# Unread 512-column products ahead of the scores in two attentions of a two-model kernel

## The chip, the cores and the metric

One Trainium2 chip, one core of it. The metric is device microseconds of one execution of the whole program; the state before is the median of three runs.

## The reference

The program computes a block of one model and then the two layers of a second one, for 256 tokens of width 1024 in float32: a mixing layer (gated linear attention, block attention, memory attention) with a hierarchical mixture of 32 experts; an even layer; an odd layer with sliding-window attention. Both later layers have modulation vectors ("ada") from a condition and a gated feed-forward part.

The change lies in the even layer, which has two attentions side by side on the same normed input:

```python
def _diff_attention(q, k, v, lam, slopes):        # 4 heads, two score maps each
    ...
        logits = jnp.einsum('bqhmd,bshmd->bhmqs', qi, k).astype(jnp.float32) * scale
        ...
        p = jax.nn.softmax(logits, axis=-1)
        a = p[:, :, 0] - lam * p[:, :, 1]
        return jnp.einsum('bhqs,bshe->bqhe', a.astype(v.dtype), v)

def _dsa_attention(q, k, v, iq, ik, iw, slopes, topk):   # 8 heads, keys chosen by an index score
    ...
        idx_logits = jnp.einsum('bqhd,bsd->bqhs', iqi, ik).astype(jnp.float32) * IDX_DIM ** -0.5
        score = jnp.einsum('bqhs,bqh->bqs', jax.nn.relu(idx_logits), iwi.astype(jnp.float32))
        score = jnp.where(causal[None], score, -jnp.inf)
        _, sel = lax.top_k(score, topk)
```

The second attends only to the chosen keys, with softmax and a distance penalty like the first.

## The kernel before, in words

Each engine has its own hand-written program; they meet at semaphores. Helpers record the instructions, so nearly all TensorE work has line 1826 (`mm`) or, for transposes, 1830 (`tr`), and nearly all VectorE and ScalarE work line 32.

*Attention as a pipeline.* An attention is a list of units. A unit is one block of 128 queries with two score maps (two maps of one head in attention 2, two heads in attention 3). A unit has 128 keys (first query block) or 256 (second). Attention 2 has eight units, alternately 128 and 256 keys; attention 3 has eight, first four with 128 keys, then four with 256. `attend(n, beside, ready)` runs `pipeline(...)`: at step t, TensorE does `turns` of unit t-3 (transposes of the softmaxed rows), `scores` of unit t and `values` of unit t-4 (product with v), in that order. VectorE at step t does `weights` of unit t-1 (adds the distance penalty, takes the row limit; waits for the scores), `norms` of unit t-2 (after ScalarE's exponential; these feed `turns`), the reading out of unit t-5, and side work.

*Banks of PSUM.* Scores of unit U go to banks 2(U%2) and 2(U%2)+1. `take(b)` waits until VectorE has read what was in the bank; the two score products read 64 rows each (rows 0 to 63 and 64 to 127 of the array).

*Side work.* `side.go(beside)` at the head of `scores` runs up to two pieces of other work: in attention 2 transposes of heads (`headturn`) and the index scores of attention 3 (`indexer`: two 64-row products, a relu by ScalarE, a weighted sum by VectorE, four times for each query block). VectorE's side work is the top-k selection (MAX8 and MATCH_REPLACE8 in rounds).

*Ada runs.* `ada(("u", n, u))` behind the scores computes modulation vectors of later stages: in units 0, 2, 4, 6 a run of eight float32 products of 512 columns (`ring,csr`, in the trace 16 instructions, four side by side at 32 columns of the array each), copied to `acc` by ScalarE; in units 1, 3, 5, 7 its closing: four float32 products of 1 column on `acc` (`ones,acc`, 8 instructions), read by VectorE into `modc`. A run waits for its weights in the ring of slots that SP's queue fills, and for VectorE's reading of bank 7.

*Operands.* `hH` (in the trace `hT_r`) holds the rounded, normed and modulated input of the layer, 8 chunks of 256 columns. After the projections nobody reads it in this layer's attentions; attention 3 writes its results to chunks 4 to 7. A product of two rounded operands is one instruction, one of two float32 operands two.

The names and lines of the change are in the TensorE program:

Of the kernel before, what the change touches and what calls it, by code (L numbers as in the profile page):

```python
# [113 lines left out]
def pipeline(n, *stages):  # L114
    for t in range(n + max(lag for lag, _ in stages)):
        for lag, stage in stages:
            if 0 <= t - lag < n:
                stage(t - lag)
# [118 lines left out]
def build(nc, A, out_ap, dbg):  # L237
    ctx = ExitStack()
    with ctx:
# [5 lines left out]
        def both(name, shape):  # L245
            with nc.sbuf_tensor(name + "_r", shape, FR) as rounded:
                pass
            return sb(name, shape), rounded
# [15 lines left out]
        hT, hH = both("hT", [128, 8, 256])  # L264
# [41 lines left out]
        _, WF = both("W_a", [128, 3072])  # L306
# [12 lines left out]
        _, WFc = both("W_c", [128, 3072])  # L319
# [4 lines left out]
        ps = [ctx.enter_context(nc.psum_tensor(f"ps{i}", [128, 512], FP)) for i in range(8)]  # L324
# [93 lines left out]
        for i in range(nch):  # L418
            if i == first["ak"]:
                last_use = {}  # L420
            b = min(range(3 if i in beside else 6), key=lambda z: (last_use.get(z, -1), z))
# [1391 lines left out]
        def tensor(pe):  # L1813
# [6 lines left out]
            def take(*banks):  # L1820
                for b in banks:
                    if b in free:
                        pe.wait_ge(*free.pop(b))

            def mm(out, lhsT, rhs, start, stop):
                return pe.matmul(out, lhsT, rhs, start=start, stop=stop, skip_group_check=True)  # L1826

            def tr(out, in_):
                n = in_.shape[0]
                return pe.transpose(out, in_, ident[0:n, 0:n])  # L1830

            def ada(point):
                for v, what in plan.rows.get(point, ()):
                    l, i, k = plan.ada_order[v]
                    take(7)
                    if what == "run":
                        w = ring[:, slot[k], :].rearrange("p (c n) -> p c n", c=8)
                        pe.wait_ge(*landed[k])
                        if v == 0:
                            pe.wait_ge(s_cs, 1)  # L1840
                        for c in range(8):
                            t = mm(ps[7][32 * (c % 4):32 * (c % 4) + 32, :], csr[:, c, :], w[:, c, :], c < 4, c >= 4)
                        t.then_inc(s_ar, 1)
                        free[7] = (s_acp, v + 1)
                        continue
                    pe.wait_ge(s_acp, v + 1)
                    if row_gate(l, i):
                        mm(ps[7][:, :], ones[:, :], acc[:, :], True, False)
                        mm(ps[7][:, :], ones[0:1, :], gates[0:1, 512 * (i % 2):512 * (i % 2) + 512], False,
                           True).then_inc(s_ac, 1)  # L1850
                        free[7] = C.next(s_gate)
                    else:
                        for n in range(4):
                            t = mm(ps[7][:, n:n + 1], acc[:, 128 * n:128 * n + 128], ones[:, 0:1], True, True)
                        t.then_inc(s_ac, 1)
                        free[7] = C.next(s_modc)
# [16 lines left out]
            def begin(i):  # L1873
                ada(("f", i))
# [117 lines left out]
            def attend(n, beside, ready):  # L1992
                at_n = attns[n]

                def scores(u):
                    U, unit = at_n.u0 + u, at_n.units[u]
                    side.go(beside)
                    if n == 3 and u == 4:
                        side.until(ev, "sel1")
                    for need in ready.get(u, ()):  # L2000
                        pe.wait_ge(*need)
                    for m in range(2):
                        b = 2 * (U % 2) + m
                        take(b)
                        mm(ps[b][:, 0:unit.nk], unit.q[m], unit.k[m], True, True).then_inc(s_sc, 1)
                        free[b] = (s_mx, 2 * U + m + 1)
                    ada(("u", n, u))

                def turns(u):
                    U, unit = at_n.u0 + u, at_n.units[u]  # L2010
                    b, n = 4 + U % 2, unit.nk // 128
                    take(b)
                    pe.wait_ge(s_nm, U + 1)
                    for i in range(unit.blocks):
                        o = 257 * (i // n) + 128 * (i % n)
                        t = tr(ps[b][:, 128 * i:128 * i + 128], at_n.pb[:, U % 4, o:o + 128])
                    t.then_inc(s_tr, 1)
                    free[b] = (s_cp, U + 1)

                def values(u):  # L2020
                    U, unit = at_n.u0 + u, at_n.units[u]
                    n, pT = unit.nk // 128, at_n.pT[:, U % 2, :]
                    if unit.first:
                        take(6)
                    pe.wait_ge(s_cp, U + 1)
                    if unit.lam is not None:
                        for i in range(n):
                            t = mm(ps[6][:, 0:128], pT[:, 128 * i:128 * i + 128], unit.v[0][i], i == 0, i == n - 1)
                        t.then_inc(s_pv, 1)
                    else:  # L2030
                        for i in range(n):
                            for m in range(2):
                                t = mm(ps[6][64 * m:64 * m + 64, 128 * unit.a:128 * unit.a + 128], unit.v[m][i],
                                       pT[:, 128 * (n * m + i):128 * (n * m + i) + 128], i == 0, i == n - 1)
                                if i == n - 1:
                                    t.then_inc(s_pv, 1)
                    if unit.last:
                        free[6] = (s_fin, at_n.fin[u])

                pipeline(len(at_n.units), (3, turns), (0, scores), (4, values))  # L2040


# [127 lines left out]
            attend(1, 1, {0: [(s_hv, 4)]})  # L2170
            side.end()
            ada(("o", 0))
            pe.wait_ge(s_gla, 8)
            pe.wait_ge(s_fin, t1.end)
# [388 lines left out]
```

## Time and profile before

| | us |
|---|---|
| median of 3 runs (1468.08 to 1469.96) | 1469.69 |
| the profiled execution | 1468.73 |
| its span, first to last instruction | 1467.0 |
| TensorE busy, whole program | 1191.2 (81%) |
| VectorE busy | 615.8 (42%) |
| ScalarE busy | 475.6 (32%) |
| mean granted clock of TensorE (1.00 is 2.4 GHz) | 0.88 |

Times in the trace are microseconds from the first instruction. PE is TensorE, PEld its weight loads, DVE VectorE, ACT ScalarE. PEclk is the mean granted clock of a stretch: 0.50 is the low level, 1.2 GHz. Matmuls overlap in a pipeline, so the cost of one in a series is the distance between starts, not its length. The chain is followed back from the last instruction, at each step to what released it.

### The profile page before, as it was taken

The page shows a single profiled execution, that of the slowest core. Times are in us where ns is not written, and L with a number is a line of the kernel's source. Part 1 is how long each engine was busy: PE and PEld are TensorE (multiplying, and loading weights), DVE is VectorE, ACT ScalarE, POOL GpSimd, SP SyncE. Part 2 cuts the span into 40 slices and gives each one's busy share as a digit, 9 for nine tenths or more (in the row PEclk, how much of TensorE's full clock was granted, in tenths as well). Part 3 has the DMA queues.
Part 4 walks back from the last instruction along what each step waited for, and adds up shares of the span by engine and source line. Part 5 has one row for each costly group of instructions (what it writes and reads, how often), then busy time and mean ns, then how long its engine had stood idle before and what let it go on. Part 6 is the DMA issues. An engine that isn't in the chain of part 4 may idle for free.

```text
span 1467.0 us, 19464 instructions
## 1 busy us (share of the span) xinstructions
PE 1191.2 (81%) x7703; PEld 874.9 (60%) x7703; DVE 615.8 (42%) x1240; ACT 475.6 (32%) x767; POOL 7.6 (1%) x54
## 2 busy tenths in 40 slices
PE   5888888575676756846897888999999978999998
PEld 4665565242332323413675438899898735999986
DVE  3473652010010000101663676655535656565553
ACT  4561621000000000002532335555433447455541
POOL 1000000000000000000000000000000000000000
PEclk9897888798888878978897678899999988999999
DMA  8542149999999999999446431865546472655520
GB/s 294 173 150 80 59 168 424 430 429 430 431 429 428 431 430 428 431 425 401 164 152 244 172 116 58 264 204 203 191 151 223 174 274 70 222 181 187 205 98 29
DMA packets 121729, 368.67 MB, mean 251 GB/s; under 512 B 9842, under 2 KB 56093, under 8 KB 110878
## 3 DMA queue, kind: packets, MB, share of 16 engines
q1 hardware_dynamic: 120556, 367.26, 65.1%
q8 instruction: 64, 1.05, 0.3%
q10 hardware_dynamic: 1074, 0.08, 0.1%
q14 instruction: 35, 0.29, 0.1%
HBM read 366.28 MB, written 1.05 MB: 250 GB/s over the span
## 4 chain that ended last, share of the span: by engine, by line
PE 57%; DMA 22%; DVE 12%; ACT 5%; issue 3%; SPq 1%; DVEq 0%; ACTq 0%
PE ps L1826 54%; DMA more<-in_w_gate_dram 8%; DMA more<-in_w_down_dram 7%; DMA more<-in_w_up_dram 6%; PE ps L1830 3%; DVE st L32 3%; DVE ring_r L32 2%; DVE R_c L32 2%; SPq L669 1%; DVE X_c L32 1%; DVE R_a L32 1%; DVE X_a L32 1%; ACT W_c_r L32 1%; ACT X_c L32 1%; DVE sc L32 1%
## 5 line engine op out<-in xcount | busy, mean ns | idle before, releaser
L1826 PE MATMUL ps<-hT_r,ring_r 128*128 128x256 f32 x864 | 243.7, 282 | 0.0
L1826 PE MATMUL ps<-ring,xg 128*32 128x512 f32 x640 | 140.1, 734 | 126.1 <-DMA more<-in_w_gate_dram 79.3
L1826 PEld LDWEIGHTS ps<-ring,xg 128*32 128x32 f32 x640 | 36.9, 132 | 222.3 <-issue 222.3
L1826 PEld LDWEIGHTS ps<-hT_r,ring_r 128*128 128x128 f32 x864 | 166.0, 192 | 0.0
L32 DVE TENSOR_TENSOR ring_r<-ring,W_c_r 128x1024 fp32r<-128x1024 f32 x94 | 115.2, 1225 | 96.3 <-ACT W_c_r L32 92.4
L1826 PE MATMUL ps<-R_c_r,W_c_r 128*128 128x256 f32 x608 | 152.7, 283 | 0.0
L32 DVE TENSOR_TENSOR ring_r<-ring,X_c_r 128x1024 fp32r<-128x1024 f32 x88 | 107.8, 1225 | 95.2 <-ACT X_c_r L32 92.3
L1826 PE MATMUL ps<-R_c_r,X_c_r 128*128 128x256 f32 x576 | 147.7, 284 | 0.0
L1826 PE MATMUL ps<-more,xg 128*32 128x512 f32 x384 | 134.6, 726 | 0.0
L32 ACT ACTIVATE W_c_r<-ring 128x1024 fp32r<-128x1024 f32 x94 | 99.7, 1060 | 87.3 <-PE ps L1826 83.0
L32 ACT ACTIVATE X_c_r<-ring 128x1024 fp32r<-128x1024 f32 x88 | 93.3, 1061 | 89.6 <-PE ps L1826 84.4
L32 DVE TENSOR_TENSOR x<-x,ps 128x512 f32<-128x512 f32 x36 | 24.8, 688 | 231.3 <-PE ps L1826 231.0
L1826 PE MATMUL ps<-hT_r,X_c_r 128*128 128x256 f32 x416 | 118.3, 284 | 2.9 <-DVE R_c_r L32 2.5
L1826 PE MATMUL ps<-hT_r,W_c_r 128*128 128x256 f32 x416 | 118.6, 285 | 1.9 <-DVE R_c_r L32 1.8
L1826 PEld LDWEIGHTS ps<-R_c_r,W_c_r 128*128 128x128 f32 x608 | 108.8, 190 | 0.0
L1826 PEld LDWEIGHTS ps<-R_c_r,X_c_r 128*128 128x128 f32 x576 | 104.0, 191 | 1.5 <-issue 1.5
L1826 PE MATMUL ps<-ring_r,hT_r 128*128 128x512 f32 (+1 forms) x240 | 94.8, 395 | 0.0
L1826 PEld LDWEIGHTS ps<-hT_r,X_c_r 128*128 128x128 f32 x416 | 78.8, 189 | 4.4 <-issue 3.0
L1826 PEld LDWEIGHTS ps<-hT_r,W_c_r 128*128 128x128 f32 x416 | 79.7, 191 | 2.7 <-DVE R_c_r L32 2.2
L1826 PE MATMUL ps<-ring,csr 128*32 128x512 f32 x384 | 63.6, 794 | 13.1 <-DVE modc L32 12.6
L1826 PE MATMUL ps<-ring,hid 128*32 128x512 f32 x320 | 60.2, 654 | 12.7 <-DMA more<-in_w_down_dram 11.6
L1826 PE MATMUL ps<-sel,hn 128*128 128x128 f32 x256 | 63.1, 410 | 2.1 <-DVE sel L32 2.1
(280 smaller groups left out, 1912.4 us busy)
## 6 DMA issues: line engine op xcount, KB each, us to landing
ring<-in_ada_w_dram SPq DMA_DIRECT2D x24, 2048.0 KB, 8.1
ring<-in_w_gate_dram SPq DMA_DIRECT2D x20, 2048.0 KB, 18.9
ring<-in_w_up_dram SPq DMA_DIRECT2D x20, 2048.0 KB, 20.0
ring<-in_w_down_dram SPq DMA_DIRECT2D x20, 2048.0 KB, 19.4
more<-in_w_gate_dram SPq DMA_DIRECT2D x12, 2048.0 KB, 27.9
more<-in_w_up_dram SPq DMA_DIRECT2D x12, 2048.0 KB, 28.4
more<-in_w_down_dram SPq DMA_DIRECT2D x12, 2048.0 KB, 27.9
ring<-in_ffn_gate_dram SPq DMA_DIRECT2D x22, 1024.0 KB, 5.9
```

What stands on the lines that cost most here:

```text
L32: op(*args, **kw).then_inc(sem, 1)
L669: sp.dma_start(dst, src).then_inc(s_w[slot[k]], 16)
L1826: return pe.matmul(out, lhsT, rhs, start=start, stop=stop, skip_group_check=True)
L1830: return pe.transpose(out, in_, ident[0:n, 0:n])
```

## The change

Ahead of each of the two score products of a unit, in attentions 2 and 3 only, three products of 512 columns go to the same bank: chunk 0 of `hH`, 128 columns wide, as the weights, chunks 0 and 1 as the 512 moving columns. The score product then overwrites the part of the bank that is read. So there are 6 per unit, 96 in all; nothing reads them. Nothing else is changed.

```diff
+            steady = hH[:, 0:2, :].rearrange("p c n -> p (c n)")
+
+            def keep(b):
+                mm(ps[b][:, :], hH[:, 0, 0:128], steady, True, True)
...
                     for m in range(2):
                         b = 2 * (U % 2) + m
                         take(b)
+                        if n in (2, 3):
+                            for _ in range(3):
+                                keep(b)
                         mm(ps[b][:, 0:unit.nk], unit.q[m], unit.k[m], True, True).then_inc(s_sc, 1)
                         free[b] = (s_mx, 2 * U + m + 1)
```

## Rows read from the trace of the kernel before

**Rows 1.** The page's chain that ended last, whole program, by engine.
```profile
PE 57%; DMA 22%; DVE 12%; ACT 5%; issue 3%; SPq 1%; DVEq 0%; ACTq 0%
```

**Rows 2.** The same chain, 787.2 to 892 us alone, by line.
```profile
by line: PE ps L1826 36.5%; DVE st L32 11.6%; DVE R_c L32 10.0%; DVE X_c L32 9.5%; issue 7.0%; PE ps L1830 5.2%; ACT R_c L32 4.6%; ACT X_c L32 3.5%; DVE s L32 2.1%; DVE hn L32 1.4%; DVE sc L32 1.3%; ACT sc L32 1.2%; DVE ring_r L32 1.2%; ACT
```

**Rows 3.** Stretches: length, busy time (instructions) of each engine, PEclk, DMA share, GB/s.
```profile
787.20:892.00 104.80, 79.40 (x407) 41.32 (x405) 67.47 (x241) 40.88 (x111) 0.69 (x2) 0.68 0.40 141
810.90:814.20 3.30, 2.57 (x19) 1.58 (x15) 0.61 (x2) 2.25 (x7) 0.00 (x0) 1.00 0.49 139
814.30:821.00 6.70, 6.70 (x30) 2.84 (x32) 5.17 (x25) 2.27 (x7) 0.29 (x1) 0.50 0.66 249
821.20:824.40 3.20, 2.20 (x18) 1.66 (x14) 2.82 (x12) 0.98 (x5) 0.00 (x0) 1.00 0.84 323
824.60:834.70 10.10, 7.64 (x24) 3.26 (x28) 6.97 (x29) 2.40 (x6) 0.00 (x0) 0.50 0.22 91
872.40:882.40 10.00, 9.07 (x72) 5.18 (x72) 6.97 (x27) 8.04 (x23) 0.00 (x0) 1.00 0.01 2
```

**Rows 4.** Timeline of TensorE, 512-column products: start, length, what.
```profile
778.72 0.63 PE L1826 MATMUL ps<-W_c_r,hT_r 128*128 128x512 f32 x1
779.14 0.63 PE L1826 MATMUL ps<-W_c_r,R_c_r 128*128 128x512 f32 x1
...
786.54 0.39 PE L1826 MATMUL ps<-X_c_r,R_c_r 128*128 128x512 f32 x1
786.77 0.39 PE L1826 MATMUL ps<-ring_r,hT_r 128*128 128x512 f32 x1
```

**Rows 5.** Timeline of TensorE in the stage, from three queries; in brackets idle before, releaser.
```profile
794.84 1.12 PE L1830 MATMUL ps<-ident,R_c 128*128 128x128 f32 x4 [4.96 <-DVE R_c L32]
...
801.07 1.86 PE L1826 MATMUL ps<-ones,acc 128*128 128x1 f32 x8
...
807.73 3.45 PE L1826 MATMUL ps<-ring,csr 128*32 128x512 f32 x16
...
826.00 2.49 PE L1826 MATMUL ps<-R_c 64*128 64x256 f32 x4 [2.23 <-DVE modc L32]
...
850.36 0.80 PE L1826 MATMUL ps<-R_c 64*128 64x128 f32 x4
851.09 3.64 PE L1826 MATMUL ps<-ring,csr 128*32 128x512 f32 x16
...
857.89 2.96 PE L1826 MATMUL ps<-ring,csr 128*32 128x512 f32 x16 [0.90 <-DVE modc L32]
...
865.26 0.48 PE L1830 MATMUL ps<-ident,X_c 128*128 128x128 f32 x2 [2.08 <-DVE X_c L32]
...
868.72 3.64 PE L1826 MATMUL ps<-ring,csr 128*32 128x512 f32 x16 [1.83 <-DVE modc L32]
...
873.03 0.70 PE L1826 MATMUL ps<-R_c 64*128 64x256 f32 x4
873.66 1.05 PE L1826 MATMUL ps<-ones,acc 128*128 128x1 f32 x8
...
876.02 1.92 PE L1826 MATMUL ps<-ring,csr 128*32 128x512 f32 x16
```

**Rows 6.** Chain pieces in order of time: start, us, what.
```profile
799.49 3.46 PE ps L1826 x12
...
813.57 1.27 PE ps L1826 x8
...
832.36 3.13 PE ps L1826 x16
...
868.72 4.01 PE ps L1826 x20
```

**Rows 7.** Chain by line, 815 to 826.1 us.
```profile
by line: DVE X_c L32 26.6%; DVE R_c L32 26.3%; DVE st L32 22.0%; issue 10.6%; PE ps L1826 7.1%; DVE s L32 6.9%; DVE modc L32 3.1%; DVE hn L32 2.7%; DVEq L30 2.1%
```

**Rows 8.** Chain by line, 850.4 to 868.7 us.
```profile
by line: DVE st L32 35.5%; DVE R_c L32 25.8%; DVE X_c L32 14.4%; issue 8.8%; DVE sc L32 7.7%; DVE s L32 2.5%; DVE modc L32 1.9%; DVEq L30 1.7%; DVE hn L32 1.6%; PE ps L1826 1.2%
```

## Prediction

> **What bounds the kernel now.** I read the page's chain first: over the whole program the work that ended last is 57% TensorE, 22% transfers, 12% VectorE [rows 1]. The transfers belong to the expert layer. The change is in one stage, from the first scores of attention 2 at 787.2 us to the end of attention 3 at 892.0, 104.8 us, so everything below is read there. I call the units a0 to a7 (attention 2) and b0 to b7 (attention 3).
>
> The chain inside the stage, grouped by line [rows 2], is mixed: TensorE (its two lines) holds 36.5 + 5.2 = 41.7% of 104.8, that is 43.7 us; most of the rest is VectorE (the index selection, the softmax work), with ScalarE's copies and exponentials. The table of stretches [rows 3] has TensorE busy for 79.4 of 104.8 us at a mean granted clock of 0.68, and the clock takes only its two levels: 0.50 (1.2 GHz) in most of the stage, 1.00 (2.4 GHz) in short pieces. It is low even where TensorE is busy all the time (814.3 to 821.0, 6.70 of 6.70 us). So this is a stage in which TensorE is slow, partly on the chain, and idle for 25.4 us. The question is how much of the added work falls on those 25.4 us, and how much low clock it turns into high.
>
> The timeline of TensorE [rows 5] says who ends the idle: 4.96 us before 794.84, 2.23 before 826.00, 2.08 before 865.26, 1.83 before 868.72, each ended by VectorE.
>
> **The change, part by part.** Nothing is removed or moved and no wait is added: the bank is taken before the unread products, as it was before the score. Per unit there are six products of 512 columns, three ahead of each of the two scores.
>
> *Price of one product.* Rounded 512-column products follow each other every 0.23 us at the high clock (786.54 to 786.77) and every 0.42 at the low one (778.72 to 779.14) [rows 4]. Loading their weights is inside that pitch. Six cost 1.39 or 2.55 us. The Trainium skill ("TensorE: Matmul & The Clock Gate", Part 1, on why a gap is longer than the columns) gives a start-to-start of 215.7 ns for 512 columns at 2.4 GHz; by it six would be 1.29 us and my sum 0.8 us smaller. The trace has 0.23, and I use that.
>
> *Price of the splitting.* The two scores of a unit use 64 rows each and now run side by side: x4 instructions in 0.70 us for 256 keys at the high clock, 0.80 for 128 keys at the low one [rows 5]. With full-height products between them they can't. A float32 product is two instructions, and the ada run shows what an instruction of 512 columns costs: 16 of them, four side by side, in 1.92 us, so 0.48 each, or 0.24 for 256 columns. A second score alone therefore adds about 0.43 us (256 keys) or 0.21 (128) at the high clock, twice that at the low.
>
> A batch so costs 1.60 or 1.82 us high and 2.98 or 3.40 low (128 or 256 keys, eight units of each): 27.4 us in all if the clock were always high, 51 if always low. It costs nothing only where TensorE waits anyway.
>
> *Where the batches lie.* I take the clock to rise where it does now: during or at the end of an ada run or a stretch as dense as one. A batch is as dense, so it brings the rise forward.
> - a0: the 4.96 us idle follows. 0.
> - a1: on the chain (3.46 us piece at 799.49 [rows 6]), low clock: 2.55 + 0.85. The closing products of 1 column after it (1.86 us low, 1.05 high [rows 5]) then run high: -0.8. **+2.6**.
> - a2: low, 2.98; its ada run of 3.45 us finishes at the high clock, about 2.1: **+1.7**.
> - a3: high, 1.82, less 0.2 of their own piece of 1.27 [rows 6], which ends at the high clock, and about 0.2 that they now wait for ScalarE's copy: **+1.4**.
> - a4, a5: from 815 to 826 the chain is VectorE's, TensorE 7.1% of it [rows 7], and TensorE then idles 2.23 us; its ada run also falls from 3.6 to 1.9. 3.4 against 2.2 + 1.7: **0**.
> - a6: low, 2.98; its ada run, 3.13 on the chain [rows 6], goes to 2.0: **+1.8**.
> - a7: high, 1.82 less 0.3 of waiting: **+1.5**.
> - b0, b1: VectorE sets this stretch (TensorE has 1.2% of the chain from 850.4 to 868.7 [rows 8]), but TensorE idles only 0.90 us before the ada run at 857.89. 2.98 at the low clock (1.60 if it rises inside b0) + 1.60, less 1.72 for the ada run between them (3.64 to 1.92) and less 0.90, is 0.6 to 2.0: **+1.5**.
> - b2, b3: under VectorE, 2.08 us idle follow: **0**.
> - b4: in the 1.83 us idle; its ada run, 3.64 low now and on the chain (the 4.01 piece [rows 6]), comes at the high clock: **-1.7**.
> - b5 to b7: TensorE runs from 872.4 to 882.4 with hardly a gap, at clock 1.00 already [rows 3, 5]; nothing can be given back. 3 x 1.82: **+5.5**.
> - the last values: perhaps a little of them at the high clock: **-0.3**.
>
> Sum: 2.6 + 1.7 + 1.4 + 1.8 + 1.5 + 1.5 - 1.7 + 5.5 - 0.3 = **+14.0 us**.
>
> *Who is behind the batches.* On TensorE's queue the ada run and the transposes of later units; behind these ScalarE's copy to acc, then the next ring slot on SP's queue. Transfers take a share of 0.40 in the stage [rows 3], so later loads shift with TensorE and cost nothing. After 892 the chain is TensorE's again, and I let the shift through whole.
>
> The profiled execution took 1468.73 us around a span of 1467.0; with 14.0 it is 1482.7. The median of the runs, 1469.69, lies 1.0 above it: **1483.7 us**, 1.0% slower.
>
> **Bounds of what no row shows.** How the clock answers is unknown. Most favourable: high throughout. The mean of 0.68 means 64% of the time at the low level; of the chain's 43.7 us, 28.0 are then low and half of them, 14.0, could be saved. The eight exposed batches (a1, a2, a3, a6, a7, b5, b6, b7) cost 5 x about 1.73 + 5.5 = 14.1 at the high clock, b0 and b1 some 0.6: +0.7 us. Least favourable: the batches run low and raise nothing, except b5 to b7, which begin high: 2 x 2.98 + 3 x 3.40 + 5.5 = 21.7; over their cover a4 and a5 6.4 - 2.2 = 4.2, b0 to b3 11.9 - 3.0 = 8.9, b4 3.4 - 1.8 = 1.6: +36. Between them I take 14.0 because the rows show both: rises after dense stretches, falls soon after in thin ones.
>
> **Rivals.**
> 1. *The clock is held high through the stage.* Then +0.7 us: 1470.4, no change. The Trainium skill says this on the same page ("Why this matters for your kernels"): keep matmuls going without idle gaps and the clock stays up. Against it by rows: at 810.9 to 814.2 the clock is high with TensorE busy 2.57 of 3.30 us and is low right after [rows 3], because that work is short scores and 1-column products; between batches there will be several us of the same.
> 2. *Fewer batches are exposed than I count* (the other side). This is rival 1 with a0 to a7 mostly under VectorE's selection: with the clock high the break-even is 14.0 / 1.7 = 8 exposed batches. With only five or six exposed it is -4: 1465.7. For it: 25.4 us of idle. Against: the chain names TensorE at a1, a3, a6 and in all of b5 to b7.
> 3. *The batches run low and raise nothing*: +36, 1505.7. For it: 814.3 to 821.0 is low at full busy. Against: the clock is high right behind it, from 821.2 [rows 3].
> 4. *All hidden*: 0 to 2 us. 27.4 us of work against 25.4 of idle, in the wrong places; nearly excluded by b5 to b7.
> That the products are dropped somewhere is no rival: each is an instruction of its own.
>
> **How the numbers follow.** Forecast 0.72 (its own range 1476 to 1490), rival 1 0.08, rival 2 0.06, rival 3 0.11, rival 4 0.03. No change means within 0.2% (2.9 us), about what a measurement of this kernel can tell. Faster 0.06; same: rival 1 and most of rival 4, 0.10; slower 0.84. The range 1474 to 1491 leaves out rivals 1, 2, most of 3 and 4 and a little of the forecast's own tails.
>
> **What the profile after would show.** 96 rounded products on hT_r alone, pitch 0.23 or 0.42, their mean clock about 0.8. Stage span 104.8 to about 119, TensorE's mean clock in it from 0.68 to 0.75 or 0.85. The piece from b5 to b7 longer by 5.5 with no gaps and the clock at 1.00: the surest step. The idle of 2.23 and 1.83 gone. The ada run of b4 at 1.92 instead of 3.64. Outside the stage nothing moves by more than 2 us. I am wrong if the stage keeps its length because the 41.7% of the chain shrinks by as much as is added, or if the batches appear at pitch 0.42 throughout.

## The result, and the profile after

The changed kernel takes 1501.01 us (median of 4 runs, 1490.43 to 1508.08), the kernel before 1469.83 in the same comparison: a ratio of 1.0197, 95% interval 1.0165 to 1.0229. So it is 2.0% slower, where 1.0% was forecast, and outside the range of 1474 to 1491. The direction was right and the size about half of what was measured. The profiled execution took 1504.22 us around a span of 1502.5, so it is 35.5 us longer than the one before.

The page after: its first line, busy time, the row of the granted clock, and the chain by engine.

```profile
span 1502.5 us, 19656 instructions
...
PE 1231.4 (82%) x7799; PEld 902.7 (60%) x7799; DVE 616.2 (41%) x1240; ACT 475.8 (32%) x767; POOL 7.6 (1%) x54
...
PEclk9897988787896897886996778899999889899999
...
PE 61%; DMA 22%; DVE 9%; ACT 4%; issue 3%; SPq 1%; DVEq 0%; ACTq 0%
```

TensorE's share of the chain rose from 57% [rows 1] to 61%; the 22% of transfers stayed. The chain of the stage alone, 791.6 to 923.7 us, by line:

```profile
by line: PE ps L1826 65.4%; DVE X_c L32 5.5%; PE ps L1830 4.5%; DVE R_c L32 4.3%; DVE st L32 4.3%; issue 4.1%; ACT R_c L32 2.1%; ACT X_c L32 2.0%; DVE s L32 1.3%; ACT sc L32 1.0%; DVE ring_r L32 0.9%; ACT acc L32 0.9%; DVE hn L32 0.9%; ACT 
```

Its two lines hold 69.9% of 132.1 us, 92 us, where they held 43.7 of 104.8 [rows 2]. A mixed stage became one that TensorE sets. The stretches (columns as in [rows 3]) and the added group (out<-in, shape, count | busy, mean ns | idle before):

```profile
791.60:923.70 132.10, 114.44 (x502) 63.03 (x501) 67.50 (x241) 40.92 (x111) 0.70 (x2) 0.76 0.32 112
826.10:836.20 10.10, 10.10 (x54) 5.65 (x54) 6.22 (x30) 3.26 (x11) 0.30 (x1) 1.00 0.58 202
856.90:865.00 8.10, 8.10 (x23) 5.30 (x23) 1.56 (x5) 0.88 (x2) 0.40 (x1) 0.50 0.35 134
880.70:911.30 30.60, 30.60 (x171) 16.66 (x168) 19.19 (x69) 12.94 (x40) 0.00 (x0) 1.00 0.41 138
```

```profile
L1826 PE MATMUL ps<-hT_r 128*128 128x512 f32 x96 | 37.5, 506 | 0.0
```

The stage grew by 27.3 us (132.1 against 104.8) at a mean clock of 0.76; TensorE idles 17.7 us in it, not 25.4. VectorE's and ScalarE's busy time is the same. The other 8.2 of the 35.5 us is a stage that starts 4.4 us later (791.6 against 787.2) and 3.8 us more behind it. So the sign "outside the stage nothing moves by more than 2 us" did not come true in this trace. I don't count either to the change all the same: of the runs below, the profiled one of attention 3 alone starts its stage at 791.4, ahead of all its products, and the profiled one of the first filling of idle time has the same extra behind the stage at a time no longer than before.

The timeline of TensorE after: four batches, two at the low clock (a1, a2), then a7 and b0 with the work behind them, then b4's ada run and b5.

```profile
804.62 1.65 PE L1826 MATMUL ps<-hT_r 128*128 128x512 f32 x3
806.20 1.22 PE L1826 MATMUL ps<-R_c 64*128 64x256 f32 x2
807.35 1.65 PE L1826 MATMUL ps<-hT_r 128*128 128x512 f32 x3
808.93 1.22 PE L1826 MATMUL ps<-R_c 64*128 64x256 f32 x2
810.08 1.86 PE L1826 MATMUL ps<-ones,acc 128*128 128x1 f32 x8
...
816.20 1.65 PE L1826 MATMUL ps<-hT_r 128*128 128x512 f32 x3
817.77 0.79 PE L1826 MATMUL ps<-R_c 64*128 64x128 f32 x2
818.50 1.65 PE L1826 MATMUL ps<-hT_r 128*128 128x512 f32 x3
820.08 0.79 PE L1826 MATMUL ps<-R_c 64*128 64x128 f32 x2
820.80 2.82 PE L1826 MATMUL ps<-ring,csr 128*32 128x512 f32 x16
...
861.17 1.22 PE L1826 MATMUL ps<-R_c 64*128 64x256 f32 x2
862.32 1.87 PE L1826 MATMUL ps<-ones,acc 128*128 128x1 f32 x8
...
877.09 3.64 PE L1826 MATMUL ps<-ring,csr 128*32 128x512 f32 x16
...
895.54 1.92 PE L1826 MATMUL ps<-ring,csr 128*32 128x512 f32 x16
...
897.95 0.94 PE L1826 MATMUL ps<-hT_r 128*128 128x512 f32 x3
898.82 0.70 PE L1826 MATMUL ps<-R_c 64*128 64x256 f32 x2
899.45 0.96 PE L1826 MATMUL ps<-hT_r 128*128 128x512 f32 x3
900.34 0.70 PE L1826 MATMUL ps<-R_c 64*128 64x256 f32 x2
900.97 1.05 PE L1826 MATMUL ps<-ones,acc 128*128 128x1 f32 x8
```

Take starts, not lengths. In b5 the batch and its two scores last from 897.95 to 900.97, 3.02 us, where the pair alone took 0.63 (873.03 to 873.66 [rows 5]): 2.39 us added, at the high clock. Six products account for 0.87 + 0.89 = 1.76 of it (forecast 1.39: the second of each three starts 0.31 to 0.34 us after the first and the score 0.33 after the third; only the step between is 0.23), and the two scores, alone, for 0.63 each instead of 0.63 together (forecast 0.43 more, measured 0.63 more). At the low clock a2's takes 816.20 to 820.80, 4.60, against 0.73 before [rows 5]: 3.87 added, forecast 2.98. a1's takes 5.46; less 1.15 for a pair at the low clock (850.14 to 851.29 in the trace of the run with six products ahead of the pair, below), that is 4.3, forecast 3.40.

### The profile page after: what moved, and what is told of

The parts are those of the page before. It is cut to its first block, busy times and chain, and to the rows that moved or that the text cites. A ratio compares the mean times of both kernels' runs of the same rounds, so it can differ in the third digit from the quotient of the medians.

```text
span 1502.5 us, 19656 instructions
## 1 busy us (share of the span) xinstructions
PE 1231.4 (82%) x7799; PEld 902.7 (60%) x7799; DVE 616.2 (41%) x1240; ACT 475.8 (32%) x767; POOL 7.6 (1%) x54
## 3 DMA queue, kind: packets, MB, share of 16 engines
HBM read 366.28 MB, written 1.05 MB: 244 GB/s over the span
## 4 chain that ended last, share of the span: by engine, by line
PE 61%; DMA 22%; DVE 9%; ACT 4%; issue 3%; SPq 1%; DVEq 0%; ACTq 0%
PE ps L1826 58%; DMA more<-in_w_gate_dram 8%; DMA more<-in_w_down_dram 7%; DMA more<-in_w_up_dram 6%; PE ps L1830 3%; DVE st L32 2%; DVE ring_r L32 2%; SPq L669 1%; DVE R_c L32 1%; DVE R_a L32 1%; DVE X_a L32 1%; ACT X_c L32 1%; DVE X_c L32 1%; ACT R_a L32 1%; DVE hn L32 1%
## 5 line engine op out<-in xcount | busy, mean ns | idle before, releaser
L1826 PE MATMUL ps<-ring,csr 128*32 128x512 f32 x384 | 60.3, 756 | 9.0 <-DVE modc L32 9.0
L1826 PE MATMUL ps<-ring,hid 128*32 128x512 f32 x320 | 54.8, 610 | 11.3 <-DMA more<-in_w_down_dram 10.4
```

## The experiments

Each experiment is compared with runs of the kernel before taken beside it; their medians are 1469.8, 1469.8 and 1469.5. All the kernels compute what the kernel before does; only products that nobody reads differ. A ratio turned into us is (ratio - 1) times that median. "Stage" is the same stretch in each one's trace: 104.8 us before.

**a0 alone.** The first batch of attention 2 only.

```diff
-                        if n in (2, 3):
+                        if n == 2 and u == 0:
```

> Six unread products ahead of the first unit of attention 2 alone, where TensorE idles 4.96 us right behind. Theory A (the cost lies where a batch is exposed on TensorE's path, and a batch with its alternation between full-height and 64-row products is dearer than I reckoned): 0, within 1 us of before. Theory B (adding products changes the rest of the program too: outside the stage the changed kernel was 4 us later before the stage and 3 us after it): 2 to 8 us slower. Theory C (the clock: units cost what I reckoned, the rest is low clock): 0.

1469.4 us, ratio 0.9982 [0.9962, 1.0002]; stage 104.81, clock 0.68. The batch lies in idle time and costs nothing, and nothing changes outside the stage either, so B is out for this batch.

**One attention at a time.**

```diff
-                        if n in (2, 3):
+                        if n == 2:
```

> The batches in attention 2 only. The profile of the changed kernel has VectorE's closing of unit a7 late by 22.4 us, of which 4.4 were there before the stage: 18.0. Theory A: +16 to +20, with a4 and a5 at 0. My prediction had +9.0 for these units. Theory B: +22 or more.

1490.42 us, 1.0121 [1.0087, 1.0155]; stage 124.98, clock 0.69.

```diff
-                        if n in (2, 3):
+                        if n == 3:
```

> The batches in attention 3 only. The changed kernel lost 31.7 - 22.4 = 9.3 us there. Theory A: +8 to +11 (b0 at the low clock about 4, b5 to b7 about 7, b4 gives 1.7 back). My prediction had +5.3 less 0.3. Theory B: +13 or more.

1482.03 us, 1.0068 [1.0047, 1.0089]; stage 119.00, clock 0.72. The two ratios sum to 1.89%, against 1.97% for both. Attention 2, for which I had counted 9.0 us, costs about 18; attention 3, for which I had 5.0, about 10. In both, the forecast is half, and both lie in the range of theory A.

The profiled execution of attention 3 alone is its slowest (1487.71 us), and its stage is 14.2 us longer. Of these, 2.3 lie ahead of the first batch: the last product ahead of b0's starts 64.35 us into the stage (855.72), where it was 62.01 (849.21), with the same instructions up to there. And the clock falls in b6, in work as dense as around it:

```profile
884.30:894.50 10.20, 10.20 (x37) 3.99 (x34) 3.80 (x13) 2.08 (x6) 0.00 (x0) 0.50 0.00 1
```

**b5 to b7 alone.** The surest step.

```diff
-                        if n in (2, 3):
+                        if n == 3 and u >= 5:
```

> The batches ahead of the last three units only, where TensorE is busy without a gap at the high clock. Price by the prediction 3 x 1.82 = +5.5. Theory A: the changed kernel shows 3.02 us from the first product of b5's batch to the closing products where there were 0.63, so 2.4 each: +6.8 to +7.2. Theory B: more than +9.

1477.88 us, 1.0045 [1.0023, 1.0067], so about 6.6 us; stage 111.42, also 6.6 more; forecast 5.5. The interval (3 us to each side) holds 5.5 and theory A's 6.8 to 7.2 alike; the trace tells them apart. A batch with its scores costs 2.39 there, but its first product starts 0.19 us behind the transposes (872.44 to 872.63), where the scores started 0.37 behind them (872.66 to 873.03); three times 2.39 - 0.18 is 6.6. TensorE never waits there and stays at the high clock. Stretch from b5's batch on:

```profile
872.60:887.30 14.70, 14.70 (x83) 8.28 (x83) 5.30 (x19) 6.99 (x21) 0.00 (x0) 1.00 0.01 2
```

**The same products, scores left side by side.** Six ahead of the first score, none between the two.

```diff
-                        if n in (2, 3):
-                            for _ in range(3):
+                        if n in (2, 3) and m == 0:
+                            for _ in range(6):
```

> All six products ahead of the first score, the two scores side by side again, all 16 units; the columns are the same 96 x 512. Theory A (a large part of the price is the alternation between full-height products and 64-row scores, 1.4 low or 0.8 high per exposed unit of 256 keys, 1.1 or 0.5 per unit of 128): about 9 us less than the changed kernel, +19 to +21 over before. Theory C (my prices hold and the rest was low clock): 4 us less at most, +24 to +27.

1482.98 us, 1.0085 [1.0059, 1.0110]. The same 96 products cost 12.5 us here and 29 in the change (0.0197 x 1469.8): 16.5 us of the 29 come with the splitting, with what it does to the clock. The 12.5 is less than either theory had expected (19 to 21, 24 to 27): the splitting is dearer still than theory A had it. Its stage, and one of its batches, at the high clock:

```profile
787.52:906.24 118.72, 97.75 (x503) 57.57 (x501) 67.44 (x241) 40.87 (x111) 0.69 (x2) 0.79 0.36 125
```

```profile
883.80 1.64 PE L1826 MATMUL ps<-hT_r 128*128 128x512 f32 x6
885.37 0.70 PE L1826 MATMUL ps<-R_c 64*128 64x256 f32 x4
886.00 1.05 PE L1826 MATMUL ps<-ones,acc 128*128 128x1 f32 x8
```

2.20 us for the same work that takes 3.02 when alternated, and the four score instructions (x4) again last 0.63.

**Eight columns instead of 512.** The alternation stays, nearly all the columns go.

```diff
-                mm(ps[b][:, :], hH[:, 0, 0:128], steady, True, True)
+                mm(ps[b][:, 0:8], hH[:, 0, 0:128], steady[:, 0:8], True, True)
```

> The same 96 products at the same places with 8 columns in place of 512: alternation and weight loads stay, the columns are gone. Theory A: +9 to +15, about half of the loss stays. Theory C, by which columns make the price: 0 to +5 (the splitting alone).

1502.43 us, 1.0213 [1.0175, 1.0251]: 31 us, not to be told from the change itself, and far above what either theory had (9 to 15, 0 to 5), since both left out what the clock would do. A 256-key batch with its scores is cheaper at the high clock (901.83 to 903.92, 2.09 us against 3.02), but the high clock is rarer:

```profile
788.07:923.26 135.19, 120.12 (x503) 73.13 (x501) 67.43 (x241) 40.89 (x111) 0.69 (x2) 0.59 0.31 109
```

```profile
901.83 0.47 PE L1826 MATMUL ps<-hT_r 128*128 128x8 f32 x3
902.24 0.70 PE L1826 MATMUL ps<-R_c 64*128 64x256 f32 x2
902.86 0.50 PE L1826 MATMUL ps<-hT_r 128*128 128x8 f32 x3
903.29 0.70 PE L1826 MATMUL ps<-R_c 64*128 64x256 f32 x2
903.92 3.59 PE L1826 MATMUL ps<-ring,csr 128*32 128x512 f32 x16
```

A mean of 0.59, below the 0.68 of before, and the ada run behind this batch lasts 3.59 us, nearly all at the low level. The 504 further columns of each product pay for themselves, and no more, by the higher clock that is seen with them (0.76 in the change).

**The splitting alone.** The kernel before with one 8-column product between the two scores of each unit.

```diff
+                        if n in (2, 3) and m == 1:
+                            keep(b)
                         mm(ps[b][:, 0:unit.nk], unit.q[m], unit.k[m], True, True).then_inc(s_sc, 1)
```

> One unread product of 8 columns between the two scores of each unit, nothing ahead of the first, 16 units. It keeps the separation of the two 64-row scores and leaves out five of six weight loads and all the columns. Theory A (separation and change of rows are the dear part): about 1.3 low and 0.7 high per exposed unit, +7 to +12 over before. Rival (it is the six weight loads of the batch that keep the price of the 8-column run up): +2 to +4.

1480.88 us, 1.0072 [1.0050, 1.0094]. Sixteen tiny products, 10.6 us, in the 7 to 12 of theory A and not the 2 to 4 of its rival (the weight loads). The clock is 0.63, below the 0.68 of before, so a part of the 10.6 is clock:

```profile
788.04:905.10 117.06, 98.29 (x422) 51.30 (x421) 67.49 (x241) 40.86 (x111) 0.69 (x2) 0.63 0.36 126
```

```profile
891.13 0.70 PE L1826 MATMUL ps<-R_c 64*128 64x256 f32 x2
891.75 0.27 PE L1826 MATMUL ps<-hT_r 128*128 128x8 f32 x1
891.96 0.70 PE L1826 MATMUL ps<-R_c 64*128 64x256 f32 x2
892.58 1.05 PE L1826 MATMUL ps<-ones,acc 128*128 128x1 f32 x8
```

From 891.13 to 892.58 is 1.45 us against 0.63 side by side [rows 5]: the second score costs 0.62 of the difference and the product 0.21.

**Twice as many.** Six products ahead of each score.

```diff
-                            for _ in range(3):
+                            for _ in range(6):
```

> Six products ahead of each score, 12 per unit. If the clock stays where it is: about 8 exposed batches at 1.4 to 2.5 more and some 4 us that no longer fit under VectorE, +42 to +48 over before. If a batch twice as long holds the clock high through the stage: the high price and up to 14 us back, +30 to +36, with the stage's mean clock over 0.9.

1507.97 us, 1.0252 [1.0213, 1.0290], 37 us, between the two ranges expected (30 to 36, 42 to 48): 96 products more cost about 8 us more than the change (the intervals overlap; the stages of the two traces differ by 11.7). At the high clock throughout they would be 22 (an estimate, 96 x 0.23); in its trace the clock goes to 0.87, not 0.76, and a part of them lies in idle time.

```profile
786.82:930.61 143.79, 127.78 (x598) 77.63 (x597) 67.42 (x241) 40.90 (x111) 0.69 (x2) 0.87 0.30 103
```

**b5 to b7, in two further forms.** Unsplit, and with eight columns.

```diff
-                        if n in (2, 3):
-                            for _ in range(3):
+                        if n == 3 and u >= 5 and m == 0:
+                            for _ in range(6):
```

> Six products ahead of the pair, in b5 to b7 only, where the clock is high. The stage with all batches ahead of the pair shows 2.20 us from the first product to the closing ones against 0.63: 1.57 a unit, +4.7. With the scores split the same three units cost +6.6. If the alternation costs nothing at the high clock: the same +6.6.

1477.36 us, 1.0045 [1.0025, 1.0065]; stage 112.23. By the batches of the traces it should be 2.4 us cheaper than the alternating form (3 x 0.82), and by the medians it is not; but their intervals reach some 3 us to each side. The traces say more. The first row is the kernel before up to b4's ada run, the second this kernel up to the same place, with the same instructions:

```profile
787.20:868.72 81.52, 60.19 (x278) 31.06 (x276) 52.16 (x194) 26.01 (x72) 0.69 (x2) 0.67 0.51 181
787.22:871.10 83.88, 61.77 (x278) 31.78 (x276) 52.20 (x194) 26.00 (x72) 0.69 (x2) 0.65 0.51 175
```

So 2.4 of the 7.4 us by which its stage is longer lie ahead of all its batches. From b4's ada run to the end of the stage it takes 28.36 us, the kernel before 23.25 and the alternating form 29.89: unsplit, the three batches cost 5.1 us, split 6.6, though b5's batch still began at the low clock here. That agrees with the runs over all sixteen units.

```diff
-                mm(ps[b][:, :], hH[:, 0, 0:128], steady, True, True)
+                mm(ps[b][:, 0:8], hH[:, 0, 0:128], steady[:, 0:8], True, True)
...
-                        if n in (2, 3):
+                        if n == 3 and u >= 5:
```

> The six products of b5 to b7 with 8 columns. With the clock staying high: six weight loads of 0.11, 0.43 for the split and about 0.4 for the changes of rows, 1.5 a unit, +4.5. If the long products were what kept the clock high there, it falls inside b5 to b7 and the three units cost +8 to +12, more than with 512 columns.

1479.28 us, 1.0065 [1.0044, 1.0087], 9.6 us, in the 8 to 12 expected if the clock falls; stage 113.27: the smallest products are no cheaper. The stretch that was at 1.00 in the first form of b5 to b7 is at 0.68, with TensorE just as busy, and b6's ada run takes 3.64 us, not 1.92:

```profile
872.50:888.60 16.10, 16.10 (x80) 9.70 (x79) 5.13 (x18) 6.99 (x21) 0.00 (x0) 0.68 0.01 2
```

```profile
879.34 1.22 PE L1826 MATMUL ps<-R_c 64*128 64x256 f32 x2
880.49 3.64 PE L1826 MATMUL ps<-ring,csr 128*32 128x512 f32 x16
```

**Products only where TensorE idles.** The kernel before, and the same 512-column product in its waits, never between the scores of a unit: 20 behind a0's ada run, 9 ahead of a6's side work, 2 in each of a6's and a7's, and 5 ahead of b4's ada run. That is 38, and the trace has 38. Seven more were written ahead of b4's values, but never issued: their condition asks for `n == 3`, and in that function `n` is the number of key blocks, 2 here. So what the expectation says of those seven wasn't tried.

```diff
+            def fill(b, count):
+                take(b)
+                for _ in range(count):
+                    mm(ps[b][:, :], hH[:, 0, 0:128], steady, True, True)
...
+                    if n == 3 and u == 4:
+                        fill(6, 5)
                     ada(("u", n, u))
+                    if n == 2 and u == 0:
+                        fill(2, 20)
```

> The kernel before with such products only where TensorE idles, none between the scores: 20 behind the ada run of a0 (4.96 us idle), 9 ahead of a6's side work (2.23 us) and 2 more in its and a7's waits for the relu, 5 ahead of b4's ada run (1.83 us), 7 ahead of the values of b4 (1.76 us). If low clock on exposed work is what costs, 3 to 7 us faster than before, with 794 to 803, 826 to 835 and the last values at the high clock. If filler in idle time buys nothing (the clock falls again before the work comes): 0, or slower by what spills over.

1467.64 us, 0.9977 [0.9955, 0.9999], 3.4 us less, at the edge of what can be told from none; stage 100.93, clock 0.79. Then with more of the waits: 3 products between the two pieces of side work of a1, a6 and a7, 6 ahead of b1's transposes, 6 instead of 5 ahead of b4's ada run: 50 in all.

```diff
+                    if n == 2 and u in (1, 6, 7):
...
+                        fill(2 * (U % 2), 3)
...
+                    if at_n is t3 and u == 1:
+                        fill(6, 6)
```

> The filler in idle time again, with 3 more products inside a1's side work, 3 in place of 2 in a6's and a7's, and 6 in the 2.08 us ahead of b1's transposes so that b4 and its ada run find the high clock. If exposed low clock is what costs: stage 98 to 100 us (104.8 before, 100.9 with the first filler), 5 to 7 us faster than before. If the extra filler spills over: no better than the first filler, -2 to -4.

1464.28 us (1461.92 to 1470.67), 0.9963 [0.9947, 0.9979]: faster than both kernels, by 5.4 us (0.37%) than the one before, as expected (5 to 7). By the marks of the others its stage is 99.2 us (786.61 to 885.84). A round 100 us over it, and its timeline around a1 and b4:

```profile
787.00:887.00 100.00, 78.90 (x460) 46.31 (x459) 67.42 (x241) 40.90 (x112) 0.69 (x2) 0.86 0.42 148
```

```profile
789.22 4.83 PE L1826 MATMUL ps<-hT_r 128*128 128x512 f32 x20
794.26 0.66 PE L1830 MATMUL ps<-ident,R_c 128*128 128x128 f32 x4 [0.22 <-DVE R_c L32]
...
798.82 1.05 PE L1826 MATMUL ps<-ones,acc 128*128 128x1 f32 x8
...
861.37 2.90 PE L1826 MATMUL ps<-hT_r 128*128 128x512 f32 x6
864.20 2.22 PE L1826 MATMUL ps<-ring,csr 128*32 128x512 f32 x16
```

The 4.96 us of idle [rows 5] are now 0.22, the transposes behind them take 0.66 us instead of 1.12, a1's closing products 1.05 instead of 1.86, and b4's ada run 2.22 instead of 3.64. TensorE is about as busy as before (78.1 us in its 99.2 against 79.4) with 50 more products in it, at 0.86 instead of 0.68.

## Why the prediction was wrong in size

**The clock of each batch against the forecast.** The shift of the stage's events on VectorE (the closing of a unit, its softmax work) from the profile before to the one after, with the common 4.4 us taken off, gives each batch its own price:

| batch | forecast | measured | what the trace shows |
|---|---|---|---|
| a0 | 0 | 0 | in idle time |
| a1 | +2.6 | +4.6 | 4.3, low; closing products 1.86, still low |
| a2 | +1.7 | +3.4 | 3.9, low; its ada run 2.82, not 2.1 |
| a3 | +1.4 | +2.2 | high |
| a4, a5 | 0 | 0 | in idle time |
| a6 | +1.8 | +2.6 | as forecast but for the price |
| a7 | +1.5 | +5.3 | low throughout, closing products 1.87 |
| b0, b1 | +1.5 | +4.3 | b0 low, ada run between them 3.64 |
| b2, b3 | 0 | 0 | in idle time |
| b4 | -1.7 | -1.6 | ada run 1.92 |
| b5 to b7 | +5.5 | +6.6 | high, no gaps |
| last values | -0.3 | 0 | |
| sum | +14.0 | +27.3 | (rows rounded) |

**The first step that failed is the price of the splitting.** I put a batch at 1.82 us (256 keys, high) and 2.98 (128 keys, low); they are 2.39 and 3.87. The term was mis-sized twice: a score alone lasts as long as two side by side (0.63, not 0.43 more), and a group of three beside 64-row work takes about 0.1 us more than the pitch of 0.23 behind its first product and again behind its last. The first could have been read before: the pair has its four instructions in 0.63 us [rows 5], two at a time, so each step is 0.31 and not the 0.24 that I took from the ada run (and two of 0.24 are 0.48, where I wrote 0.43). By these prices the exposed batches come out 6.4 us dearer: 0.9 (a1), 0.9 (a2), 0.55 (a3), 0.9 (a6), 0.55 (a7), 1.5 (b0 and b1), 1.1 (b5 to b7, whose first products start 0.18 earlier than the scores did). The price itself is shown at 0.82 us for a unit of 256 keys at the high clock (3.02 against 2.20). Over all units the split also shifts the clock: without it the same products cost 12.5 us in place of 29, and the split with hardly a column costs 10.6.

**The second is where I took the clock as high.** "a7: high" and "less 1.72 for the ada run between them" fell: a7 ran low (1.9 us more for the batch, 0.5 for the pair of scores itself and 0.8 for its closing products), b0's ada run took 3.64 (1.7 more), and the two gains at a1 and a2 (0.8 and 0.7) did not come. That is 6.4. With the other 6.4 it makes 12.8 of the 13.3 us between forecast and trace; the rest, 0.5, I can't assign.

The rise that I assumed ("a batch is as dense, so it brings the rise forward") came at two of the five batches that began low: a2's ada run lasts 2.82 us instead of 3.45 and a6's 1.92 instead of 3.08. At a1, a7 and b0 it did not: from 856.90 to 865.00 TensorE is busy for 8.10 of 8.10 us and granted 0.50 throughout. The Trainium skill ("TensorE: Matmul & The Clock Gate", "Why this matters for your kernels") advises to avoid idle between matmul bursts. Products in the idle time did raise the mean to 0.86, which agrees. That stretch of 8.10 us, the 10.20 us of attention 3 alone, and the 0.68 of b5 to b7 with eight columns, do not: there was no idle and the clock was low. What the engine did in those stretches is 64-row scores, ada runs, and products of few columns or one between the full ones. Which of these matters, I did not try apart, so why the clock stayed low is open.

**The rivals.** Rival 1 (clock high, +0.7) is out: at most 0.87 was reached, with twice the products, and that cost 37 us. Rival 2 (five or six exposed batches) is out: those that cost something are a1, a2, a3, a6, a7, b0 with b1, and b5 to b7. Rival 3 (low throughout, +36) was nearer than I gave it credit for; the truth lies between it and my forecast, with a1, a2, a6, a7 and b0 low and a3, b1 and b5 to b7 high. Rival 4 is out.

**What held.** The hidden units, b4's gain, and the stretch from b5 to b7 at 1.00 with no gap are as stated (the last not in every trace: in that of attention 3 alone the clock fell in b6). The idle of 1.83 us ahead of b4's ada run is gone, as forecast. That of 2.23 us ahead of 826.00 [rows 5] is not: at the same scores, now at 840.58, TensorE still waits 1.50 us.

**What stays open.** The time of the changed kernel varies from 1490 to 1508 us over four runs, and I have no profile of a short run. The kernel before varies too, from 1467.4 to 1480.9 over the 29 runs beside the first experiments, so four runs don't show that the change widens the spread. That other rises and falls of the clock make the difference is argued, not shown; two traces do show an unchanged part of the stage 2.3 to 2.4 us longer. The account by batches above is that of one execution. Nor is the split between "columns" and "clock" exact, since each kernel sets its own clock.

## What to carry to other kernels

Work that nobody reads is worth adding where TensorE waits and real work follows at the low clock, and nowhere on its path: 50 products in the idle stretches gave 5.4 us back, 96 ahead of the scores cost 29. Never put a full-height product between two that use half of the rows and run side by side: price such an insertion by the distance from start to start of the alternated series, since the second of the pair costs as much as the first. And where the clock steps between two levels, cost an added batch at the low level unless the trace shows the high one at that place before and behind, and allow for the low one even then (b6 of attention 3 alone).

## What the runs showed of the hardware that I had not expected

- A product of 8 columns between scores costs the kernel as much as one of 512: 1.0213 [1.0175, 1.0251] against 1.0197 [1.0165, 1.0229]. The batches are shorter and the clock lower (0.59 against 0.76).
- Changing between full-height and 64-row products has a price that no pitch of either shows: starts 0.31 to 0.34 us apart instead of 0.23 at the high clock, and each of two scores parted by a product takes the 0.63 us of both together.
- A busy TensorE was granted the low clock for 8.10 us on end in a dense mix of scores and products, and in another run for 10.20 us on end, right behind 23.8 us at the high one with no idle either.
- The same instructions took 83.88 us in one execution and 81.52 in another, at a mean clock of 0.65 and 0.67.
- With twice the added products the mean clock was 0.87, not 0.76, and the 96 more cost only about 8 us.
